# Three float32r passes for the projections of an MLA layer, with the latent and the keys turned elsewhere in the order

## The reference, cut to what matters

```python
down = rmsnorm(x, kv_norm_g) @ kv_w_down            # 1024 -> 256 + 32
c_kv = rmsnorm(down[..., :256], kv_a_norm_g)
k_rope = apply_rope(down[..., 256:], cos, sin)      # one for all heads
up = (c_kv @ kv_w_up).reshape(B, T, 16, 64 + 64)    # k_nope and v
c_q = rmsnorm(h @ q_w_down, q_norm_g)               # h = rmsnorm(x, norm_g), 1024 -> 384
q = (c_q @ q_w_up).reshape(B, T, 16, 64 + 32)       # q_nope and q_rope, the latter rotated
```

## Time and profile before

| | us |
|---|---|
| median of 3 runs | 1514.64 (1512.64 to 1514.97) |
| the profiled execution, its own time | 1508.34 |
| its span, first to last instruction | 1506.5 |
| TensorE busy | 1409.9 (94%) |
| VectorE busy | 900.7 (60%) |
| ScalarE busy | 626.5 (42%) |
| granted TensorE clock, mean | 0.971 |

### The profile page before, as it was taken

The page is one execution under the profiler, slowest core; times in us unless marked ns, Lnnn a source line. Parts: engine busy times, 40 slices in busy tenths (PEclk is TensorE's granted clock), DMA queues, the critical chain, the costliest instruction groups (busy, mean ns, idle before and its releaser), DMA issues.

```text
span 1506.5 us, 21947 instructions
## 1 busy us (share of the span) xinstructions
PE 1409.9 (94%) x8660; PEld 1228.1 (82%) x8660; DVE 900.7 (60%) x1579; ACT 626.5 (42%) x953; POOL 61.1 (4%) x45
## 2 busy tenths in 40 slices
PE   5999999989999897989999898889999998999998
PEld 3885998789999656889999677679999767889997
DVE  6277456667676513577676566665555667475553
ACT  2332221253343326653433455653433457454331
POOL 0002000000000001100000002000000023000000
PEclk9999998999999899999999899899999999999999
DMA  6423101145654133265555243075642213376420
GB/s 219 171 79 112 57 2 57 57 168 197 202 187 143 43 119 112 65 233 178 189 175 176 72 169 135 34 285 204 223 177 103 99 51 111 112 280 224 179 100 28
DMA packets 110796, 208.11 MB, mean 138 GB/s; under 512 B 3808, under 2 KB 53088, under 8 KB 110208
## 3 DMA queue, kind: packets, MB, share of 16 engines
q1 hardware_dynamic: 110720, 207.06, 39.3%
HBM read 205.99 MB, written 1.05 MB: 137 GB/s over the span
## 4 chain that ended last, share of the span: by engine, by line
PE 85%; DVE 7%; ACT 5%; issue 2%; DMA 0%; SPq 0%; DVEq 0%; ACTq 0%
PE ps L819 19%; PE ps L739 12%; PE ps L805 10%; PE ps L800 10%; PE ps L795 9%; PE ps L1034 4%; PE ps L717 3%; PE ps L855 3%; PE ps L866 2%; ACT Ah L1403 1%; PE ps L1157 1%; PE ps L1266 1%; PE ps L1145 1%; DVE arena L2367 1%; PE ps L692 1%
## 5 line engine op out<-in xcount | busy, mean ns | idle before, releaser
L1413 ACT CAST Ah<-ringA 128x2048 fp32r<-128x2048 f32 x76 | 145.1, 1909 | 281.3 <-PE ps L805 266.9
L1979 DVE TENSOR_TENSOR Al<-ringA,Ah 128x2048 fp32r<-128x2048 f32 x76 | 174.2, 2292 | 85.5 <-ACT Ah L1413 85.2
L795 PE MATMUL ps<-hTh,Ah 128*128 128x256 f32 x1216 | 169.7, 281 | 5.3 <-DVE hTl L1964 5.1
L800 PE MATMUL ps<-hTl,Ah 128*128 128x256 f32 x1216 | 170.8, 283 | 0.4 <-DVE hTl L1964 0.3
L805 PE MATMUL ps<-hTh,Al 128*128 128x256 f32 x1216 | 169.4, 282 | 0.0
L795 PEld LDWEIGHTS ps<-hTh,Ah 128*128 128x128 f32 x1216 | 159.3, 188 | 11.7 <-issue 5.6
L1986 DVE TENSOR_TENSOR Bl<-ringB,Bh 128x1024 fp32r<-128x1024 f32 (+1 forms) x76 | 127.0, 1671 | 53.8 <-ACT Bh L1422 53.8
L800 PEld LDWEIGHTS ps<-hTl,Ah 128*128 128x128 f32 x1216 | 156.4, 190 | 0.8 <-DVE hTl L1964 0.8
L805 PEld LDWEIGHTS ps<-hTh,Al 128*128 128x128 f32 x1216 | 155.2, 190 | 0.0
L1422 ACT CAST Bh<-ringB 128x1024 fp32r<-128x1024 f32 (+1 forms) x76 | 107.3, 1412 | 111.8 <-PE ps L819 108.6
L819 PE MATMUL ps<-Bh,hidh 128*128 128x512 f32 x432 | 134.3, 392 | 4.5 <-issue 3.0
(11 more groups left out here) (354 smaller groups left out, 2042.2 us busy)
## 6 DMA issues: line engine op xcount, KB each, us to landing
ringA<-in_ffn_w_in SPq DMA_DIRECT2D x44, 1024.0 KB, 6.8
ringA<-in_mlp_w SPq DMA_DIRECT2D x32, 1024.0 KB, 7.6
ringB<-in_mlp_w SPq DMA_DIRECT2D x32, 1024.0 KB, 6.8
ringB<-in_ffn_w_out SPq DMA_DIRECT2D x44, 512.0 KB, 4.1
ringA<-in_diff_w_in SPq DMA_DIRECT2D x12, 1024.0 KB, 6.8
ringA<-in_dsa_w_in SPq DMA_DIRECT2D x8, 1024.0 KB, 6.3
ringA<-in_w_k SPq DMA_DIRECT2D x4, 1024.0 KB, 8.6
ringA<-in_w_r SPq DMA_DIRECT2D x4, 1024.0 KB, 6.2
```

The costliest lines, as they stand in the source:

```text
L795: mm(o, Ah[:, half, k * T + j * P:k * T + j * P + P], hTh[:, k, :], start=(k == 0), stop=False)
L800: mm(o, Ah[:, half, k * T + j * P:k * T + j * P + P], hTl[:, k, :], start=False, stop=False)
L1413: nc.scalar.copy(a_split(w, Ah, half), a_half(w, ap, half)).then_inc(ah_rdy, 1)
L1979: V.tensor_tensor(a_split(w, Al, half), a_half(w, (a_at[w] + par) % 2, half), a_split(w, Ah, half).bitcast(F32), ALU.subtract).then_inc(al ...
```

## The change

- The six weight pieces (kvd, qd, two halves of kvu, two slots of qu; table `MW`) are rounded by ScalarE (`round_m`) and their rests made in place by VectorE (`rest_m`). `down` and `up` replace `token_jobs`: three float32r passes (high\*high, low\*high, high\*low).
- The g_kv copy of the turned tokens becomes `h2h` (all eight by ScalarE) and `h2l` (all eight by VectorE), then `turned_split("n1")` makes `hTh` and `hTl`. ScalarE waits for `h2l` ahead of `hTh`, so the two engines take the banks one after the other. `late_norm` now waits for each token tile by itself and stands ahead of these copies.
- `kv_w_up` leaves ringA and is loaded to ringB slot 0 as soon as ffn0 has its last sum. The later pieces of ringA move up one slot.
- The latent is turned between the second and the third pass of qd, the query latent between the two halves of kvu.
- The keys are turned in two groups of eight heads, after each half of qu, into banks 0 to 3, and VectorE copies them. The queries are rotated four heads at a time and turned after that in four groups, which ScalarE copies.

```diff
+            load_a(a_at["kvd"])
+            load_a(a_at["qd"])
+            sp.wait_ge(m_rdy, 2 * (MI["ffn0"] + 1))
+            v = kview("kv_w_up", 2048)
+            for k in range(2):
+                sp.dma_start(kvuf[:, k * 2048:(k + 1) * 2048], v[:, k, :]).then_inc(dn["kvu"], 16)
+            for i in range(a_at["qu"], a_at["ffn1"]):
...
+            def down(i, b0, w, hi, lo, hi_rdy, lo_rdy):
...
+                pe.wait_ge(dn["hi"], i + 1)
+                for left, right, rdy in ((hi, wh, hi_rdy), (lo, wh, lo_rdy), (hi, wl, None)):
+                    if rdy is None:
+                        if i == 1:
+                            small_turn(0, m_ckvn, 2, 1)
+                        pe.wait_ge(dn["lo"], i + 1)
+                    for t in range(NT):
+                        for k in range(KT):
+                            if rdy is not None and t == 0 and k % 2 == 0:
+                                pe.wait_ge(rdy, n0 + k // 2 + 1)
+                            last = mm(ps[:, b0 + t, 0:w], left[:, k, t * P:(t + 1) * P], right[:, k, :],
...
+            down(0, 0, KV_LORA + QK_ROPE, h2h, h2l, dn["h2"], dn["l2"])
+            down(1, 2, Q_LORA, hTh, hTl, ha_rdy, hv_rdy)
+            pe.wait_ge(dn["hi"], 4)
+            pe.wait_ge(dn["th"], 1)
             for s in range(2):
+                up(J["kvu"][0] + 4 * s, 512, [1024 * s, 1024 * s + 512], ckvTh, ckvTl, kvuh,
+                   [kvul[:, 0:2048], kvul[:, 2048:4096]], (1, 4))
+                if s == 0:
+                    small_turn(2, m_cqn, 3, 2)
+            pe.wait_ge(dn["th"], 2)
+            for s in range(2):
+                pe.wait_ge(dn["hi"], 5 + s)
...
+                up(J["qu"][0] + 4 * s, 384, [0, 384], cqTh, cqTl, wh, wl, (2, 5 + s))
+                if s == 0:
+                    pe.wait_ge(job_out, J["kvu"][0] + 8)
+                    pe.wait_ge(dn["rope"], 1)
+                keys_turn(4 * s)
+            for q in range(4):
+                pe.wait_ge(job_out, J["qu"][0] + 2 * q + 2)
+                pe.wait_ge(dn["rope"], 2 * q + 3)
+                turn_blocks(J["qt1"][0] + 2 * q, [((lambda t, h=h: m_q[:, t, h, :]), QD)
+                                                  for h in range(4 * q, 4 * q + 4)])
...
+            def round_m(i, rdy, n):
+                act.wait_ge(rdy, n)
+                nc.scalar.copy(MW[i][0], MW[i][1]).then_inc(dn["hi"], 1)
+            act.wait_ge(f1_rdy, 2 * (G0["ffn0"] + NCH["ffn0"]))
+            round_m(0, a_loaded[a_kvd], 32 * (a_at["kvd"] // 2 + 1))
             res_root(1)
+            round_m(1, a_loaded[a_qd], 32 * (a_at["qd"] // 2 + 1))
...
-            turned("n1", "g1_mix", "g_kv")
             late_norm("n1")
+            for b in range(4):
+                act.wait_ge(tp_rdy, 4 * TI["n1"] + b + 1)
+                for k in (2 * b, 2 * b + 1):
+                    last = A_(h2h[:, k, :], ps[:, tbank("n1", b), (k % 2) * T:(k % 2) * T + T],
+                              ACT.Copy, scale=col("g_kv", k))
+                last.then_inc(dn["h2"], 1)
+            act.wait_ge(dn["l2"], 4)
+            turned_split("n1", "g1_mix")
...
+                scaled(m_down[:, t, :], ps[:, t, 0:288], t).then_inc(dn["out"], 1)
+            for k in range(2):
+                round_m(2 + k, dn["kvu"], 32)
             root("ckv", st[:, 18:20], st[:, 16:18], KV_LORA, eps)
...
+            latent(1, 0, ckvTh, "kv_a", 2)
             for t in range(NT):
...
+            round_m(4, a_loaded[a_qu[0]], 32 * (a_at["qu"] // 2 + 1))
             root("cq", st[:, 22:24], st[:, 20:22], Q_LORA, eps)
             j = J["kvu"][0]
             for q in range(4):
+                if q == 2:
+                    round_m(5, a_loaded[a_qu[1]], 32 * ((a_at["qu"] + 1) // 2 + 1))
+                    latent(2, 2, cqTh, "q_n", 3)
...
+            def rest_m(i):
+                dve.wait_ge(dn["hi"], i + 1)
+                V.tensor_tensor(MW[i][2], MW[i][1], MW[i][0].bitcast(F32), ALU.subtract
+                                ).then_inc(dn["lo"], 1)
             res_norm(1, "g0_fres", "n1")
+            rest_m(0)
```

```diff
+            def keys_out(s0):
+                for s in range(s0, s0 + 4):
+                    dve.wait_ge(dn["kt"], s + 1)
+                    V.tensor_copy(m_KT[0:QD, 2 * s:2 * s + 2, :].rearrange("p h t -> p (h t)"),
+                                  ps[0:QD, s % 4, :]).then_inc(dn["kto"], 1)
+            for q in range(4):
+                if q % 2 == 0:
+                    keys_out(2 * q)
+                for t in range(NT):
+                    dve.wait_ge(job_out, J["qu"][0] + 2 * q + t + 1)
...
+                    rotate(m_q[:, t, hs, 64:80], m_q[:, t, hs, 80:96], (c1, s1, s1, c1),
+                           quarters(m_rt[:, 256 * t:256 * t + 256], 4, 16), done=dn["rope"])
```

More of the change, by code:

```diff
@@ L230, in program @@
                 "ix", "ixr", "ixs"]}
+        dn = {n: sem("dn_" + n) for n in
+              ["hi", "lo",
+               "h2", "l2",
+               "pe", "out",
+               "turn", "th", "tl", "kt", "kto",
+               "kvu", "rope"]}
         def kview(name, w):
@@ L1105, in _, with small_turn @@
             ffn("ffn0", 1)
-            def small_turn(j0, src, kts, n):
+            def small_turn(b0, src, kts, n):
                 pe.wait_ge(pre["tsm"], n)
[L1111 to L1118, removed]
+                for k in range(kts):
+                    for t in range(NT):
+                        o = (k % 2) * T + t * P
+                        last = nc.tensor.transpose(ps[:, b0 + k // 2, o:o + P],
+                                                   src[:, t, k * P:(k + 1) * P], ident)
+                last.then_inc(dn["turn"], 1)
@@ new lines, in up @@
+            def up(j0, w, cols_, hi, lo, wh, wl, n):
+                for left, right, rdy in ((hi, wh, None), (lo, wh, dn["tl"]), (hi, wl, dn["lo"])):
+                    if rdy is not None:
+                        pe.wait_ge(rdy, n[0] if rdy is dn["tl"] else n[1])
+                    for j in range(4):
+                        if rdy is None:
+                            job_bank(j0 + j)
+                        t, o = j % 2, cols_[j // 2]
+                        for k in range(len(wh)):
+                            last = mm(ps[:, bank(j0 + j), 0:w], left[:, k, t * P:(t + 1) * P],
+                                      right[k][:, o:o + w],
+                                      start=(right is wh and left is hi and k == 0),
+                                      stop=(right is wl and k == len(wh) - 1))
+                        if right is wl:
+                            last.then_inc(job_rdy, 1)
@@ L1120, in turn_blocks, with keys_turn @@
+            def keys_turn(s0):
+                for s in range(s0, s0 + 4):
+                    if s >= 4:
+                        pe.wait_ge(dn["kto"], s - 3)
+                    for i in range(4):
+                        h, t = 2 * s + i // 2, i % 2
+                        last = nc.tensor.transpose(ps[0:QD, s % 4, i * P:(i + 1) * P],
+                                                   m_k[:, t, h, :], ident)
+                    last.then_inc(dn["kt"], 1)
             def turn_blocks(j0, blocks):
@@ L1686, in _ @@
             prime(ACT.Exp)
[L1687 to L1692 removed]
+            for s in range(8):
+                job(J["qt1"][0] + s, lambda p: nc.scalar.copy(
+                    m_QT[0:QD, 2 * s:2 * s + 2, :].rearrange("p h t -> p (h t)"), p[0:QD, :]))
             attend(0, m_soft)
@@ L1867, in _ @@
             empty_halves(d_QZ, 1)
-            pool.wait_ge(pre["src"], 2)
+            pool.wait_ge(pre["src"], 1)
             for half in range(2):
```

148 lines of the change are left out of this document (89 added, 59 removed).

## The result

| | before | after |
|---|---|---|
| median of the runs, us | 1514.81 (1512.64 to 1515.07, 4 runs) | 1495.78 (1494.44 to 1499.25, 4 runs) |
| ratio, 95% interval | | 0.988 (0.9863 to 0.9897) |
| profiled execution (its span), us | 1508.34 (1506.5) | 1494.65 (1492.8) |
| ffn0's last hidden rest to the first score matmul, us | 81.70 (508.67 to 590.37) | 64.57 (508.43 to 573.00) |

The change makes the kernel 19.0 us faster by the medians (15.6 to 20.8 by the interval); 1498.5 was forecast. The last line holds the edited stage alone; I call it **the stretch** and read the experiments by it. It lost 17.1 us. In a second profile of the changed kernel (e11) it was 64.46, where whole executions of one program differed by several us. **The long stretch** runs from the same rest to the next residual add and takes in the attention: 136.27 before, 119.14 and 119.04 in the two profiles after.

A forecast was written before the change was run, and what follows sets the result against it. TensorE's matmuls and waits were taken to bound the stage from first projection to first score. Savings of 7.0 matmul, 1.95 start and 7.4 turns, copies and rotations made 16.3 us: median 1514.6 to 1498.5, range 1493.5 to 1506.5.

The forecast's parts named there:

- Matmul prices: Four projections: each float32r matmul takes 133, 174 or 230 ns at 288, 384 or 512 columns, at full clock.
- The line through 328 and 512 columns: Price estimate from three-pass matmuls in the trace, 151 and 234 ns: 0.45 ns per column, for widths not in it.
- The start: First projection matmul at 520.65 instead of 522.60, 1.95 us earlier, after x's squares, root and two copies.
- The blocks: Stage from first projection matmul to first score, laid out as 9.7 + 8.9 + 11.8 + 12.5 + 3.9 + 6.6 = 53.4 us.
- The tail: After qu and key turns: VectorE's four PSUM copies and four rotations set the end, 6.6 us, attention at 574.2.
- The tight places: Cover before TensorE would wait: latent's norm 0.2 us, second qu slot 0.9, query latent 1.9.
- The queue rival: VectorE and ScalarE queues slip at the tight places; gain only 10 to 12 us, 1503 in all; chance 0.18.
- Half clock through both down projections: Low clock lasts through kvd and qd, costing 10.5 us; gain 5.8, 1509 in all; chance 0.06.
- Attention at half clock: Turns and idle time at the stage's end let the clock fall, costing some 3 us; 1501 in all; chance 0.05.
- Splits in series: Roundings and rests, 28.6 us, are exposed ahead of TensorE's passes; 12 us slower, 1527 in all; chance 0.04.
- Widths 288 and 384 at the price of 512: Matmuls of kvd, qd and qu cost 234 ns like 512 columns; 12 us less gain, 1510; chance 0.03.
- The whole time: Stage 16.3 us shorter, later stages shift unchanged; median 1514.6 becomes 1498.3, held as 1498.5.

The follow-up runs named there:

- e11: The changed kernel again, unedited, run beside e10; stretch 64.46 us, median 1495.23 us, ratio 0.989.
- e7: Changed kernel, but ScalarE copies the high tokens of kvd before it squares x for the norm; stretch 63.70 us, 1494.95 us in all.
- e6: Changed kernel, but VectorE rotates queries 8 to 11 ahead of its last four key copies and ScalarE loads the table earlier; stretch 62.90 us, 1494.21 in all.
- e3: Changed kernel, but ScalarE rounds the second half of kvu twice, ahead of the latent's root; stretch 66.77 us, 1500.09 in all.
- e5: Changed kernel, but ScalarE copies all key banks and VectorE none; stretch 64.70 us, 1496.73 in all.
- e9: Changed kernel with only the high*high pass; the rests are still computed and waited for; stretch 60.32 us, 1489.78 in all.
- e2: Changed kernel, but the latent is turned after qd's third pass, not before it; stretch 65.96 us, 1494.06 in all.
- e4: Changed kernel with 2.3 us of extra VectorE work ahead of the rest of the first qu slot; stretch 64.87 us, 1498.63 in all.
- e10: Changed kernel with the start of e7 and the tail of e8 together; stretch 60.82 us, median 1491.47 us, ratio 0.9857.
- e12: e7 with twelve plain float32 matmuls of constants filling TensorE's idle time between the query turns; stretch 63.01 us, 1490.64 in all.
- e8: e6, and ScalarE copies the last two key banks; stretch 61.98 us, 1495.71 in all.
- e1: Changed kernel's new order with whole float32 matmuls, one pass and no splits; stretch 72.38 us, 1503.41 in all.

## Why the prediction was right, step by step

**Matmul prices: right.** 133, 172.5 and 226 ns against 133, 174 and 230, or 176, 232 and 175 over the whole blocks. The line through 328 and 512 columns held on both widths that the trace of before didn't have. For 512 columns the row says 234, and I put in 230 without a reason. The price per column is then 1.35 for kvu, below the 1.36 to 1.40 that I gave.

**The start: right.** First matmul at 520.34 against 520.65; counted from the hidden rest it came 2.0 us earlier, against 1.95. It did hang on the square of x ahead of the copies, as laid out: e7 moved it, and TensorE's idle time of 0.42 us there was gone.

**The blocks.** From the chain and the windows, forecast in brackets: kvd 9.06 us (9.7), qd with the latent's turn 8.8 (8.9), kvu with the query latent's turn 11.7 (11.8), qu with the key turns 16.0 (16.4), tail 7.07 (6.6); 52.7 in all (53.4). The terms that were mis-sized: kvd by 0.6, as the clock came up during 525 and not at 527; the key turns, two groups of 1.7 us where I had 3.9 in all; the tail by 0.5 the other way. That kvd came out this near is partly luck, since the same program took 8.66 to 9.83 us for it in eight profiles. By kind the gain was 7.3 us of matmul time, 2.0 of start and 7.8 of turns, copies and rotations, where I had 7.0, 1.95 and 7.4. Some 1.2 of the 7.8 is the half clock of the kernel before's turns, for which my sum had no term.

**The tail: right in size, incomplete in mechanism.** I had "four PSUM copies at 0.6" and rotations at 1.03 each by VectorE as what sets the end. The copies took 0.60 from start to start and the rotations 0.93. The copies began 1.1 us before the end of qu's block, not 1.5, and from the end of the last rotation to the first score it took 1.96 us, not 1.6 (eight turns, then two copies in a row of which I had counted one). What the schedule didn't use is VectorE's 1.80 us of idle time ahead of its copies, which is what e6 gained by.

**The tight places: right.** 0.2 us at the norm of the latent was forecast and read. That the cover came out as forecast, with everything around it 1 us earlier than laid out, is luck; that this is the tight place is not. e3 shows what would have happened had it slipped. The queue rival failed by its margin, not in its mechanism.

**The other rivals.** Half clock through both down projections: it lasted to 526 here and to 531 in e5, and reached qd in e9 alone. Attention at half clock: it did not come in the changed kernel, but 0.05 was too little for it, since it came in e2, e3, e4 and e7. By the last turns and the time from the first score to the residual add it cost 0.8 (e4) to 2.8 us (e3); between e7 and e12 the long stretch differs by 1.9. I had 3. The Trainium skill, page "TensorE: Matmul & The Clock Gate", section on the PE-mode transpose, says that the full clock does not engage for transposes. By that rule the clock should have fallen in the changed kernel's tail, and it did not; nor did e10's, where turns alone fill TensorE from 566 to 571. In the kernel before the clock even came up, from 0.50 at 582 to 1.00 at 584, while TensorE did nothing but turns. These traces disagree with the rule, as far as it is meant for such float32 turns; they list them as MATMUL and don't show a mode. In e7 the clock fell, with turns and gaps between them. The fillers of e12 were real matmuls, so they don't tell the gaps from the turns. Splits in series: the changed kernel's groups show no such wait. In e9 they are in series: the passes that cover them are gone there. Widths 288 and 384 at the price of 512: refuted by the pitches.

**The whole time.** The stretch gave 17.1 us where 16.3 was forecast, the medians 19.0 in the first comparison and 17.4 in the second (1512.66 - 1495.23); both intervals hold 17. The profiled executions differ by 13.7 only. The starts of the residual adds show where the rest went: the changed kernel was 17.4 us ahead at 627.57 and 17.3 ahead at 970.96, then 14.6 at 1161.22. In the MLP between them TensorE stood almost still for 3 us and then ran at a lower clock, by windows of the changed kernel:

```profile
992.00:995.00 3.00, 0.07 (x1) 0.11 (x1) 2.93 (x5) 2.88 (x3) 0.00 (x0) 1.00 0.99 362
995.00:999.00 4.00, 4.00 (x13) 3.12 (x14) 4.00 (x2) 0.00 (x0) 0.00 (x0) 0.67 0.19 30
```

Counted from the same residual add, the kernel before had 1.15 us of busy time in the first of these windows, and the full clock in the second. The second profile of the changed kernel lacked most of this loss, so I put it down to that execution and not to the change. No run tests that.

## What to carry to other kernels

When a matmul is made cheaper by passes that need split operands, lay out each vector engine's queue in time and look for the one small operation that stands behind a large split (here a root of 0.29 us behind 3.70 us of rounding): its cover decides, not the sum of the added work. At the end of such a stage look for an idle wait in front of ready work (VectorE's 1.80 us), and split the last PSUM copies over both engines instead of giving them all to one (e8 against e6). Read the granted clock of every window before a cause is given to a difference: the same program's kvd differed by up to 1.2 us by the clock alone. Where whole executions scatter by more than the effect, compare a stretch between two fixed instructions, and a second, longer one that shows whether the gain is kept.

## What the runs showed of the hardware that I had not expected

- A step of 3.3 to 3.6 us that no edit made. The residual add ahead of the stage came at 314.1 to 314.7 us in before, the changed kernel, e2, e6, e7, e11 and e12, and at 317.5 to 318.1 in e1, e3, e4, e5, e8, e9 and e10, though the code up to there is the same in all of the variants. It goes with the clock. From 150 to 170 us TensorE was busy for 19.3 us in each, and the mean granted clock was 0.91 in all seven that came early and 0.83 in all seven that came late, 1.6 us by itself (20 x 0.08); from 230 to 310 it was 0.91 against 0.85 to 0.89. The profiles of e11 and e10:

```profile
150.00:170.00 20.00, 19.32 (x172) 18.43 (x171) 8.56 (x22) 6.05 (x11) 0.00 (x0) 0.91 0.28 106
150.00:170.00 20.00, 19.32 (x159) 18.47 (x159) 8.60 (x23) 6.05 (x11) 0.00 (x0) 0.83 0.31 106
```

So the same code is granted different clocks in different executions. It fits that e8 took 1495.71 us in all with a stretch 2.6 us shorter. What decides it is not shown.
- Less TensorE work does not shorten a stage in proportion. In e9 the two passes left out would take some 25 us at full clock by the changed kernel's pitches ((32 x 133 + 32 x 172.5 + 32 x 226 + 48 x 172.5) ns), and only 4.25 were gained, with waits for the rests and the clock at 0.50 from 521 to 540, from 545 to 550 and from 568 to 571.
- The clock fell between the query turns of e7, and the long stretch was 1.9 us longer than in e12, twice the gain of the edit. In e12 matmuls that compute nothing stood in the gaps and the clock stayed up; that they are the cause is not shown.
- In the kernel before the clock fell to half after a wait of 5.1 us and came back within 4 us, under turns alone.
